# Where the slots of two weight rings begin in the on-chip memory

## The chip, the cores and the metric

The kernel runs on one core of one Trainium2 chip. The metric is the device time of one execution in microseconds (us), from the first to the last instruction and what lies around them. Engines: PE is TensorE, which multiplies (PEld is its loading of the stationary operand), DVE is VectorE, ACT is ScalarE, POOL is GpSimd, SP is SyncE, which here only issues transfers.

## The reference, cut to what matters

The kernel computes four transformer layers in a row on one sequence of 256 rows and width 2048, all in float32: two layers of a first kind (modulated norm, a wide projection, sliding-window attention, spatial gating and gated linear attention side by side, an output projection), then two of a second kind (a wide projection, two attentions, two up projections, an output projection, a layer norm). By far the most arithmetic lies in the projections:

```python
proj = h @ w_in                                   # first kind, twice
out = y @ w_out
h = jnp.einsum('bsd,dc->bsc', x, w_in)            # second kind, twice
up_a = jnp.einsum('bsw,wd->bsd', out_a * jax.nn.silu(za), w_up_a)
up_b = jnp.einsum('bsw,wd->bsd', out_b * jax.nn.silu(zb), w_up_b)
y = jnp.einsum('bsd,de->bse', g_a * up_a + g_b * up_b, w_out)
```

## The kernel before, in words

**The stream of weights.** All projection weights are cut into granules of 128 partitions x 1024 float32 (`GK` = 2 blocks of `CW` = 512 columns; 512 KB each). There are 912 granules: 240 in the first block (`first_block`, from line 1100 on), 672 in the second (`second_block`). Granule n goes through slot n % 4 (`SLOTS`) of three rings in the on-chip memory: SP's queue brings it into `raw` (or, in part of the first block, into `mraw`), ACT rounds it into `whi` (`hi`, L318 and L1414), DVE subtracts to get the rest into `wlo` (`lo`, L435 and L1639), both of type float32r. The activations are split into a high and a low part in the same way (`xhi`, `xlo`, `ahi`, `alo`, `hhi`, `hlo`).

**The products.** For each granule PE runs 12 matmuls (L781 and L2173): high activation by `whi`, low activation by `whi`, high activation by `wlo`, each for two blocks of 128 weight rows and two halves of the 256 sequence rows. In each of them the 128x128 piece of the activation is stationary, and 512 columns of the slot, 2048 bytes on every partition, are the moving operand; the output goes to PSUM and is summed there. So of every 12 matmuls 8 read `whi` and 4 read `wlo`, and 912 x 12 = 10944 matmuls read the two rings.

**What sets the order.** Each engine has its own list of instructions in a fixed order, joined by semaphores: ACT waits for the transfer and for PE's last reading of the slot (`s_used`), DVE waits for ACT (`s_hi`), PE waits for both (`s_hi`, `s_lo`), SP's queue waits for DVE before it refills `raw`. Small attention products and transposes are put between granules by hand (`fills2`, `units2`). Chunk by chunk, PSUM is emptied by ACT and DVE.

**Where things lie.** Tensors are laid out one behind the other in the order of their declarations in `program` (L2274 to L2278). `border` (384 bytes for each partition) brings `x` to a multiple of 512 bytes, and since `x`, `ident`, `raw`, `whi` and `wlo` are multiples of 512 bytes long, all slots begin at multiples of 512. Of the tensors behind the rings, the big ones begin at multiples of 512 too; `sgl` begins 32 bytes behind a multiple of 64.

Of the kernel before, what the change touches and what calls it, by code (L numbers as in the profile page):

```python
# [16 lines left out]
F32 = mybir.dt.float32  # L17
F32R = mybir.dt.float32r
U32 = mybir.dt.uint32
I32 = mybir.dt.int32  # L20
ACT = mybir.ActivationFunctionType
# [3 lines left out]
P = 128  # L25
# [4 lines left out]
CW = 512  # L30
NCW = D // CW
GK = 2
SLOTS = 4
LINE = 128
NEG = -1.0e30
DEPTH = 2

# [12 lines left out]
def at(layer, per_layer, count):  # L50

    return layer * per_layer + count
# [83 lines left out]
def second_block(nc, ctx, x, rings, ps, dram, s_w, ident):  # L136


    raw, whi, wlo = rings
# [7 lines left out]
    def sem(name):  # L147
        return ctx.enter_context(nc.semaphore(name))
# [38 lines left out]
    s_hi = sem("c_hi")  # L187
# [122 lines left out]
    def _(act):  # L310
        act.wait_ge(s_mem, 2)

        for l in range(DEPTH):

            def hi(n, l=l):
                act.wait_ge(s_w[n % SLOTS], at(l, 16 * GRAN2 // SLOTS, 16 * (n // SLOTS + 1)))
                act.wait_ge(s_used, at(l, GRAN2, n + 1))
                act.activation(whi[:, n % SLOTS, :], raw[:, n % SLOTS, :], ACT.Copy).then_inc(s_hi, 1)  # L318

            def fill_hi(name, l=l):  # L320
                h, _, bank = split_views(name)
# [54 lines left out]
            for c in range(nch):  # L376
                prev, j = CHUNKS2[c - 1] if c else (None, None)
                for g in range(granules2(c)):
                    if c == 0 and (l == 0 or g >= LEAD):
                        fill_hi(("x", g))  # L380
                    if c or l == 0 or g > LEAD:
                        hi(FIRST2[c] + g)
                    if (c, g) == (F_CHUNK - 1, 0):

                        act.wait_ge(s_fw, at(l, 32, 32))
                        act.activation(wfhi[:], wf[:], ACT.Copy).then_inc(s_fwh, 1)
                    for grp, r in group_step(c, g):
                        attention(grp, r)
                    if prev == "g" and g == 4:

                        act.wait_ge(*acc_read(l, c - 1))
                        t = (y if j < NCW else gb)[:, :, (j % NCW) * CW:(j % NCW + 1) * CW]
                        act.activation(t, t, ACT.Sigmoid).then_inc(s_gate, 1)
                    if prev == "u" and j >= NCW and g == 5:
                        fill_hi(("y", 2 * (j - NCW)))
                        fill_hi(("y", 2 * (j - NCW) + 1))
                    if (c, g) == (F_CHUNK, 7):

                        act.wait_ge(s_f, l + 1)
                        act.activation(fe[:], fe[:], ACT.Exp).then_inc(s_fln, 1)  # L400
                        act.wait_ge(s_fln, at(l, 2, 1))
                        act.activation(fe[:], fe[:], ACT.Ln, bias=1.0).then_inc(s_fln, 1)
            if l < DEPTH - 1:
                for g in range(LEAD):
                    hi(g, l + 1)
# [5 lines left out]
            if l < DEPTH - 1:  # L411
                hi(LEAD, l + 1)

    @block.vector
    def _(dve):
# [9 lines left out]
        for l in range(DEPTH):  # L425
# [6 lines left out]

            def lo(n, l=l):
                dve.wait_ge(s_hi, at(l, GRAN2, n + 1))
                dve.tensor_tensor(wlo[:, n % SLOTS, :], raw[:, n % SLOTS, :], whi[:, n % SLOTS, :].bitcast(F32),  # L435
                                  ALU.subtract).then_inc(s_lo, 1)

            def fill_lo(name, l=l):
# [51 lines left out]
            def turn():  # L490

                for g in range(LEAD):
                    lo(g, l + 1)
                last_residual(0)
                variance(0)
                inverse_deviation(0)
                normalised(0, 0, CW).then_inc(s_xn, 1)
                last_residual(1)
                fill_lo(("x", 0), l + 1)
                variance(1)  # L500
                inverse_deviation(1)
                normalised(1, 0, CW).then_inc(s_xn, 1)
                link(normalised(0, CW, CW))
                fill_lo(("x", 1), l + 1)
                normalised(1, CW, CW).then_inc(s_xn, 2)
                lo(LEAD, l + 1)
# [123 lines left out]
            for c in range(nch):  # L630
                prev, j = CHUNKS2[c - 1] if c else (None, None)
                for g in range(granules2(c)):
                    if c == 0 and (l == 0 or g >= LEAD):
                        fill_lo(("x", g))
                    if c or l == 0 or g > LEAD:
                        lo(FIRST2[c] + g)
# [218 lines left out]
def rope_tables():  # L855

    half = HD // 2
    inv = (np.float32(10000.0) ** (-np.arange(half, dtype=np.float32) / half)).astype(np.float32)
    ang = (np.arange(SEQ, dtype=np.float32)[:, None] * inv[None, :]).astype(np.float32).astype(np.float64)
    t = np.stack([np.cos(ang), np.sin(ang), -np.sin(ang)])  # L860
    t = np.stack([t * SCALE2, t]).reshape(2, 3, TB, P, half).transpose(3, 0, 1, 2, 4)
    return np.ascontiguousarray(t.astype(np.float32))


def band(weight):

    t, s = np.arange(P)[:, None], np.arange(SEQ)[None, :]
    return np.concatenate([weight(t - s[:, :P]), weight(t + P - s)], axis=1).astype(np.float32)


def constants():
# [5 lines left out]

        "mask_a": band(lambda d: np.where(count(d) > 0, np.log(np.maximum(count(d), 1)), NEG)),
        "mask_b": band(lambda d: np.where(d >= 0, 0.0, NEG)),
        "tables": rope_tables(),  # L880
# [124 lines left out]
def ring_slot(item):  # L1005

    if item in ITEM:
        return ITEM[item] % RING
    return item[1] % SLOTS
# [78 lines left out]
def first_block(nc, ctx, x, rings, ps, dram, ident, s_next=None):  # L1088

    raw, whi, wlo = rings  # L1090
# [7 lines left out]
    def sem(name):  # L1098
        return ctx.enter_context(nc.semaphore(name))
# [59 lines left out]
    s_hi = sem("b_hi")  # L1159
# [142 lines left out]
    def slot(item):  # L1302

        i = ring_slot(item)
        return raw[:, i, :] if i < SLOTS else mraw[:, i - SLOTS, :]

    def landed(item):

        return s_w[ring_slot(item)], 16 * ring_uses(item)
# [99 lines left out]
    def _(act):  # L1409
        def hi(n):  # L1410
            act.wait_ge(*landed(("w", n)))
            if n >= SLOTS:
                act.wait_ge(s_used, n - SLOTS + 1)
            act.activation(whi[:, n % SLOTS, :], slot(("w", n)), ACT.Copy).then_inc(s_hi, 1)  # L1414

        def fill_copy(name, dst, rows=P, n=CW):
            act.wait_ge(*filled(name))
# [68 lines left out]
        for l in range(DEPTH):  # L1486
# [3 lines left out]
            for r in range(GRAN1):  # L1490
                if l and h_fill(l, r) is not None:
                    fill_hi(("h", l, h_fill(l, r)))
                if l == 0 or r >= AHEAD:
                    hi(GRAN1 * l + r)
# [74 lines left out]
                for grp, b in enumerate(R_SWA):  # L1569
                    if 5 <= r - b <= 7:  # L1570
# [3 lines left out]
                        w = P if u == 0 else SEQ  # L1574
                        h0, n = max(0, 2 * (u - 1)), CW // w
# [44 lines left out]
            for r in range(AHEAD if l + 1 < DEPTH else 0):  # L1620
                hi(GRAN1 * (l + 1) + r)
# [6 lines left out]
    def _(dve):  # L1628
# [7 lines left out]

        def lo(n):
            dve.wait_ge(s_hi, n + 1)
            dve.tensor_tensor(wlo[:, n % SLOTS, :], slot(("w", n)), whi[:, n % SLOTS, :].bitcast(F32),  # L1639
                              ALU.subtract).then_inc(s_lo, 1)  # L1640

        def fill_lo(name):
# [170 lines left out]
        for l in range(DEPTH):  # L1813
# [5 lines left out]
            for r in range(GRAN1):  # L1819
# [9 lines left out]
                if l == 0 or r >= AHEAD:  # L1829
                    lo(GRAN1 * l + r)  # L1830
# [135 lines left out]
            for r in range(AHEAD if l + 1 < DEPTH else 0):  # L1966
                lo(GRAN1 * (l + 1) + r)
# [218 lines left out]
def first_constants():  # L2186
# [7 lines left out]
    for m in LEVELS[1:]:  # L2194
# [8 lines left out]
        "lmask": np.stack(masks, axis=1).astype(np.uint8),  # L2203
        "mask_w": band(lambda d: np.where((d >= 0) & (d < WINDOW), 0.0, NEG)),
    }
# [63 lines left out]
def program(nc, dram):  # L2269
    with ExitStack() as ctx:  # L2270
        def sb(name, shape, dt=F32):
            return ctx.enter_context(nc.sbuf_tensor(name, shape, dt))

        sb("border", [P, LINE // 4 * 3])  # L2274
        x = sb("x", [P, TB, D])
        ident = sb("ident", [P, P])
        rings = (sb("raw", [P, SLOTS, GK * CW]), sb("whi", [P, SLOTS, GK * CW], F32R),
                 sb("wlo", [P, SLOTS, GK * CW], F32R))  # L2278
        acc = [ctx.enter_context(nc.psum_tensor(f"acc{i}", [P, TB, CW], F32)) for i in range(2)]
        psT = ctx.enter_context(nc.psum_tensor("psT", [P, TB, CW], F32))  # L2280
        psS = ctx.enter_context(nc.psum_tensor("psS", [P, TB, CW], F32))
        s_w = [ctx.enter_context(nc.semaphore(f"c_w{i}")) for i in range(SLOTS)]
        with ExitStack() as first:
            first_block(nc, first, x, rings, (acc, psT, psS), dram, ident, s_w)
        with ExitStack() as second:
            second_block(nc, second, x, rings, (acc, psT, psS), dram, s_w, ident)
# [22 lines left out]
```

## Time and profile before

| | |
|---|---|
| time of the kernel before, median of 2 runs | 2888.41 us (2887.61 to 2889.22) |
| span of the profiled execution, first to last instruction | 2885.3 us |
| PE busy with matmuls | 2799.2 us, 97% |
| DVE busy | 1792.4 us, 62% |
| ACT busy | 1375.3 us, 48% |
| mean granted TensorE clock | 0.986 |
| read from HBM | 599.41 MB, 208 GB/s over the span |

For the profiled execution the span is known and not a time of its own; the span is 3.1 us shorter than the median of the runs, which is what lies around the instructions. Matmuls overlap in the pipeline of PE: the duration of one is longer than the distance from its start to the next one's start, and it is the distance that counts for the time. The granted clock is 1.00 at 2.4 GHz and 0.50 at 1.2 GHz.

### The profile page before, as it was taken

How to read it: one execution, taken by the hardware profiler on the slowest of the kernel's cores; microseconds unless marked ns; L12 is line 12 of the kernel's file. 1: busy time of each engine (PE TensorE's matmuls, PEld its weight loads, DVE VectorE, ACT ScalarE, POOL GpSimd, SP SyncE). 2: the span in 40 equal slices, each digit the busy share in tenths (PEclk: the TensorE clock that was granted, in tenths of full speed). 3: DMA queues.
4: the chain of work that ended last, by engine and by line, in shares of the span. 5: the costliest groups of instructions: out<-in, count | busy, mean ns of one | idle time of the engine just before them, and what ended most of it. 6: DMA issues, size and time to landing. Idle time of an engine off the chain costs nothing.

```text
span 2885.3 us, 35735 instructions
## 1 busy us (share of the span) xinstructions
PE 2799.2 (97%) x13346; PEld 2318.4 (80%) x13346; DVE 1792.4 (62%) x2195; ACT 1375.3 (48%) x1785; POOL 36.0 (1%) x69
## 2 busy tenths in 40 slices
PE   6799998999998999999999999999999999999998
PEld 5678786888887888888888888878888888888886
DVE  6979898768755555555445556575565545445565
ACT  4355545555544444443545544345445445545443
POOL 0000000000000000000000000000000000000000
PEclk8999999999999999999999999999999999999999
DMA  9987697865554555465554455644555655555564
GB/s 382 354 286 254 208 357 299 314 230 183 201 200 154 173 177 178 160 224 195 177 181 169 173 198 192 222 164 169 176 173 171 224 192 172 179 176 174 197 215 146
DMA packets 159991, 603.73 MB, mean 209 GB/s; under 512 B 18376, under 2 KB 18576, under 8 KB 154464
## 3 DMA queue, kind: packets, MB, share of 16 engines
q1 hardware_dynamic: 155376, 583.08, 57.7%
q0 software_dynamic: 4464, 18.55, 2.1%
q8 instruction: 106, 1.74, 0.2%
q14 instruction: 45, 0.37, 0.0%
HBM read 599.41 MB, written 2.14 MB: 208 GB/s over the span
## 4 chain that ended last, share of the span: by engine, by line
PE 68%; DVE 1%; DMA 0%; ACT 0%; issue 0%; SPq 0%; ACTq 0%; DVEq 0%
PE acc L781 63%; PE psT L729 2%; PE psS L762 1%; PE psS L752 1%; PE psT L735 1%; PE psS L769 0%; DMA raw<-in_w 0%; DVE wlo L435 0%; ACT whi L318 0%; DVE x L488 0%; PE psT L725 0%; DVE x L487 0%; DVE x L469 0%; DVE x L471 0%; DVE stats L454 0%
## 5 line engine op out<-in xcount | busy, mean ns | idle before, releaser
L435 DVE TENSOR_TENSOR wlo<-raw,whi 128x1024 fp32r<-128x1024 f32 x672 | 822.6, 1225 | 866.1 <-ACT whi L318 863.9
L318 ACT ACTIVATE whi<-raw 128x1024 fp32r<-128x1024 f32 x672 | 711.2, 1059 | 995.8 <-PE acc L781 981.7
L781 PE MATMUL acc<-whi,xhi 128*128 128x512 f32 x2304 | 637.8, 398 | 2.5 <-DVE xlo L441 1.5
L781 PE MATMUL acc<-whi,xlo 128*128 128x512 f32 x2304 | 619.4, 390 | 0.0
L781 PE MATMUL acc<-wlo,xhi 128*128 128x512 f32 x2304 | 619.3, 390 | 0.0
L781 PEld LDWEIGHTS acc<-whi,xlo 128*128 128x128 f32 x2304 | 433.1, 188 | 92.4
L781 PEld LDWEIGHTS acc<-wlo,xhi 128*128 128x128 f32 x2304 | 433.1, 188 | 91.5
L781 PEld LDWEIGHTS acc<-whi,xhi 128*128 128x128 f32 x2304 | 422.9, 188 | 83.5 <-DVE xlo L441 3.5
L1414 ACT ACTIVATE whi<-raw 128x1024 fp32r<-128x1024 f32 x177 | 186.9, 1058 | 269.0 <-PE acc L2173 177.7
L2173 PE MATMUL acc<-whi,hhi 128*128 128x512 f32 x864 | 249.5, 411 | 31.3 <-DVE hlo L1650 31.3
L1639 DVE TENSOR_TENSOR wlo<-raw,whi 128x1024 fp32r<-128x1024 f32 x177 | 215.2, 1223 | 90.0 <-ACT whi L1414 89.3
L2173 PE MATMUL acc<-whi,hlo 128*128 128x512 f32 x864 | 238.0, 398 | 0.0
L2173 PE MATMUL acc<-wlo,hhi 128*128 128x512 f32 x864 | 236.5, 396 | 0.0
L2173 PEld LDWEIGHTS acc<-whi,hhi 128*128 128x128 f32 x864 | 159.2, 194 | 69.8 <-DVE hlo L1650 34.8
L2173 PEld LDWEIGHTS acc<-whi,hlo 128*128 128x128 f32 x864 | 166.4, 193 | 36.9
L2173 PEld LDWEIGHTS acc<-wlo,hhi 128*128 128x128 f32 x864 | 165.8, 192 | 35.9
L1414 ACT ACTIVATE whi<-mraw 128x1024 fp32r<-128x1024 f32 x63 | 66.6, 1058 | 81.7 <-PE acc L2173 61.8
L781 PE MATMUL acc<-whi,ahi 128*128 128x512 f32 x384 | 103.2, 391 | 0.0
L781 PE MATMUL acc<-wlo,ahi 128*128 128x512 f32 x384 | 102.7, 389 | 0.0
L781 PE MATMUL acc<-whi,alo 128*128 128x512 f32 x384 | 102.7, 389 | 0.0
L1639 DVE TENSOR_TENSOR wlo<-mraw,whi 128x1024 fp32r<-128x1024 f32 x63 | 77.1, 1223 | 37.7 <-ACT whi L1414 37.5
L1664 DVE SCALAR_TENSOR_TENSOR raw<-raw,crow 128x1024 f32<-128x1024 f32 x79 | 97.1, 1229 | 0.9 <-DMA raw<-in_w_late 0.2
(321 smaller groups left out, 2136.0 us busy)
## 6 DMA issues: line engine op xcount, KB each, us to landing
raw<-in_w SPq DMA_DIRECT2D x849, 512.0 KB, 3.4
raw<-in_w_late SPq DMA_DIRECT2D x79, 512.0 KB, 5.1
mraw<-in_w SPq DMA_DIRECT2D x63, 512.0 KB, 4.8
mraw<-in_w_late SPq DMA_DIRECT2D x49, 512.0 KB, 4.6
b_y<-in_w_early SPq DMA_DIRECT2D x12, 1024.0 KB, 8.4
mraw<-in_w_early SPq DMA_DIRECT2D x7, 1024.0 KB, 8.8
scr<-in_w_early SPq DMA_DIRECT2D x7, 1024.0 KB, 8.8
sgl<-in_w_early SPq DMA_DIRECT2D x6, 1024.0 KB, 9.2
```

Source lines behind the costliest of these rows:

```text
L318: act.activation(whi[:, n % SLOTS, :], raw[:, n % SLOTS, :], ACT.Copy).then_inc(s_hi, 1)
L435: dve.tensor_tensor(wlo[:, n % SLOTS, :], raw[:, n % SLOTS, :], whi[:, n % SLOTS, :].bitcast(F32), ALU.subtract).then_inc(s_lo, 1)
L729: t = pe.transpose(bank[:, k * SEQ + tb * P:k * SEQ + (tb + 1) * P], src[:, tb, col + k * P:col + (k + 1) * P], ident[:])
L735: t = pe.transpose(bank[:, k * P:(k + 1) * P], prob[:, name[2], k * P:(k + 1) * P], ident[:])
L752: m = pe.matmul(out, qT[:, h, tb * P:(tb + 1) * P], kT[:, h, 0:w], start=True, stop=True)
L762: m = pe.matmul(bank[:, h * HD:(h + 1) * HD], probT[:, u, col * P:(col + 1) * P], v[:, s, h * HD:(h + 1) * HD], start=(s == 0), stop=(s == ...
L781: m = pe.matmul(acc[c % 2][:, tb, :], a[:, kk, tb * P:(tb + 1) * P], b[:, n % SLOTS, k * CW:(k + 1) * CW], start=(kk == 0 and q == 0), sto ...
L1414: act.activation(whi[:, n % SLOTS, :], slot(("w", n)), ACT.Copy).then_inc(s_hi, 1)
L1639: dve.tensor_tensor(wlo[:, n % SLOTS, :], slot(("w", n)), whi[:, n % SLOTS, :].bitcast(F32), ALU.subtract).then_inc(s_lo, 1)
L1664: dve.scalar_tensor_tensor(out=slot(("m", i)), in0=slot(("m", i)), scalar=1.0, in1=crow[:, part * MOD_W:(part + 1) * MOD_W], op0=ALU.mult, ...
L2173: m = pe.matmul(bank_a(gc)[:, tb, :], a[:, kt, tile], b[:, n % SLOTS, k * CW:(k + 1) * CW], start=(g == 0 and k == 0 and q == 0), stop=(g ...
```

## The change

Each slot of `whi` and `wlo` becomes 8 bytes longer on every partition (`SHIFT` = 2 float32). Nothing is read or written in these 8 bytes: the two instructions that fill a slot name its first 1024 elements, and the matmuls did so before. So the four slots of `whi` begin 0, 8, 16 and 24 bytes behind a multiple of 512. `whi` as a whole is 32 bytes longer, and the slots of `wlo` begin 32, 40, 48 and 56 bytes behind a multiple of 64. The second half of a slot begins 2048 bytes behind the first, so it has the same place within 64 bytes. A new filler `border_w` of 448 bytes rounds the 64 added bytes up to 512: all that lies behind the rings moves by exactly 512 bytes, and `raw` and what lies ahead of it doesn't move. The instructions of every engine, their order and their waits are the same as before.

```diff
+SHIFT = 2
...
-                act.activation(whi[:, n % SLOTS, :], raw[:, n % SLOTS, :], ACT.Copy).then_inc(s_hi, 1)
+                act.activation(whi[:, n % SLOTS, 0:GK * CW], raw[:, n % SLOTS, :], ACT.Copy).then_inc(s_hi, 1)
...
-                dve.tensor_tensor(wlo[:, n % SLOTS, :], raw[:, n % SLOTS, :], whi[:, n % SLOTS, :].bitcast(F32),
+                dve.tensor_tensor(wlo[:, n % SLOTS, 0:GK * CW], raw[:, n % SLOTS, :], whi[:, n % SLOTS, 0:GK * CW].bitcast(F32),
                                   ALU.subtract).then_inc(s_lo, 1)
...
-            act.activation(whi[:, n % SLOTS, :], slot(("w", n)), ACT.Copy).then_inc(s_hi, 1)
+            act.activation(whi[:, n % SLOTS, 0:GK * CW], slot(("w", n)), ACT.Copy).then_inc(s_hi, 1)
...
-            dve.tensor_tensor(wlo[:, n % SLOTS, :], slot(("w", n)), whi[:, n % SLOTS, :].bitcast(F32),
+            dve.tensor_tensor(wlo[:, n % SLOTS, 0:GK * CW], slot(("w", n)), whi[:, n % SLOTS, 0:GK * CW].bitcast(F32),
                               ALU.subtract).then_inc(s_lo, 1)
...
-        rings = (sb("raw", [P, SLOTS, GK * CW]), sb("whi", [P, SLOTS, GK * CW], F32R),
-                 sb("wlo", [P, SLOTS, GK * CW], F32R))
+        rings = (sb("raw", [P, SLOTS, GK * CW]), sb("whi", [P, SLOTS, GK * CW + SHIFT], F32R),
+                 sb("wlo", [P, SLOTS, GK * CW + SHIFT], F32R))
+        sb("border_w", [P, 112])
```

## Rows read from the trace of the kernel before

**Rows 1.** The page: busy time of the engines, and the granted clock by slices

```profile
PE 2799.2 (97%) x13346; PEld 2318.4 (80%) x13346; DVE 1792.4 (62%) x2195; ACT 1375.3 (48%) x1785; POOL 36.0 (1%) x69
...
PEclk8999999999999999999999999999999999999999
```

**Rows 2.** The page: the chain that ended last, by engine

```profile
PE 68%; DVE 1%; DMA 0%; ACT 0%; issue 0%; SPq 0%; ACTq 0%; DVEq 0%
```

**Rows 3.** Groups by line: PE matmuls on the rings (count; busy us, mean ns)

```profile
L781 PE MATMUL acc<-whi,xhi 128*128 128x512 f32 x2304 | 637.8, 398 | 2.5 <-DVE xlo L441 1.5 <-ACT whi L318 0.9
...
L2173 PE MATMUL acc<-whi,hhi 128*128 128x512 f32 x864 | 249.5, 411 | 31.3 <-DVE hlo L1650 31.3
...
L781 PE MATMUL acc<-whi,ahi 128*128 128x512 f32 x384 | 103.2, 391 | 0.0
...
L2173 PE MATMUL psS<-whi,hhi 128*128 128x512 f32 x64 | 17.1, 389 | 0.0
...
L2173 PE MATMUL psT<-whi,hhi 128*128 128x512 f32 x32 | 8.6, 389 | 0.0
```

**Rows 4.** Chain in order of time, 2200 to 2400 us: start, length, what

```profile
2209.01 163.23 PE acc L781 x720
```

**Rows 5.** Windows: length, busy us (instructions) of each engine, clock, DMA share, GB/s

```profile
0.00:165.00 165.00, 122.50 (x466) 95.49 (x467) 128.11 (x157) 67.72 (x86) 11.49 (x24) 0.89 0.92 359
165.00:500.00 335.00, 316.96 (x1682) 262.14 (x1681) 295.40 (x493) 177.20 (x287) 6.91 (x12) 0.97 0.78 279
...
2211.00:2371.00 160.00, 160.00 (x708) 132.53 (x707) 83.50 (x74) 73.10 (x70) 2.70 (x5) 1.00 0.61 203
...
67.90:71.80 3.90, 3.90 (x10) 2.97 (x9) 3.52 (x15) 0.00 (x0) 0.00 (x0) 0.50 0.88 346
```

**Rows 6.** Timeline of PE at granted clock 0.50: start us, us, what

```profile
69.24 1.91 PE L2173 MATMUL acc<-whi,hlo 128*128 128x512 f32 x4
70.95 1.87 PE L2173 MATMUL acc<-wlo,hhi 128*128 128x512 f32 x4
72.65 1.09 PE L2173 MATMUL acc<-whi,hhi 128*128 128x512 f32 x4
```

**Rows 7.** Timeline of PE: matmuls of 256 moving float32r columns

```profile
2205.56 0.28 PE L769 MATMUL psS<-xhi,wflo 128*12 128x256 f32 x1
...
2208.73 0.28 PE L769 MATMUL psS<-xlo,wfhi 128*12 128x256 f32 x1
```

**Rows 8.** Timeline, 2300 to 2306 us: one granule in its turn

```profile
2301.35 1.07 PE L781 MATMUL acc<-whi,ahi 128*128 128x512 f32 x4
...
2301.61 1.06 ACT L318 ACTIVATE whi<-raw 128x1024 fp32r<-128x1024 f32 x1 [1.66 <-PE acc L781]
...
2302.70 1.23 DVE L435 TENSOR_TENSOR wlo<-raw,whi 128x1024 fp32r<-128x1024 f32 x1 [1.49 <-ACT whi L318]
...
2304.07 1.07 PE L781 MATMUL acc<-whi,ahi 128*128 128x512 f32 x4
```

**Rows 9.** Groups by line: DVE and ACT on slots, and DVE on sgl

```profile
L435 DVE TENSOR_TENSOR wlo<-raw,whi 128x1024 fp32r<-128x1024 f32 x672 | 822.6, 1225 | 866.1 <-ACT whi L318 863.9
L1639 DVE TENSOR_TENSOR wlo<-raw,whi 128x1024 fp32r<-128x1024 f32 x177 | 215.2, 1223 | 90.0 <-ACT whi L1414 89.3
...
L1919 DVE TENSOR_TENSOR b_stage<-b_stage,sgl 128x1024 f32<-128x1024 f32 x2 | 2.5, 1226 | 0.1
...
L1657 DVE SCALAR_TENSOR_TENSOR mraw<-mraw,crow 128x2048 f32<-128x2048 f32 x7 | 16.0, 2288 | 0.0
L1657 DVE SCALAR_TENSOR_TENSOR sgl<-sgl,crow 128x2048 f32<-128x2048 f32 x6 | 13.7, 2288 | 0.0
```

**Rows 10.** Groups by line: ACT on the slots

```profile
L318 ACT ACTIVATE whi<-raw 128x1024 fp32r<-128x1024 f32 x672 | 711.2, 1059 | 995.8 <-PE acc L781 981.7 <-DMA raw<-in_w 14.0
```

## The prediction

> **What bounds the kernel now.** I read the page first: PE is busy for 2799.2 us of a span of 2885.3 us, 97%, and the granted clock is nearly full throughout [rows 1]. The chain that ended last is PE's wherever it can be put down to an engine [rows 2]. No other engine comes near: DVE is at 62%, ACT at 48%. Then I asked what PE spends its time on. The groups by line give the counts: 2304, 864, 384, 64 and 32 matmuls of the kind high activation by `whi`, 3648 together [rows 3], and as many of each of the two other kinds, so 10944. Each streams 512 columns out of a slot of `whi` or `wlo`. All that the change can do to the bound lies in how long one of these streams takes.
>
> The duration in the group rows, 390 to 411 ns, is a latency and not the price. The price is the distance between starts. The chain in order of time has a piece of 720 such matmuls with nothing between them in 163.23 us, 226.7 ns each, or 2.72 us for a granule of 12 [rows 4, 8]. 10944 x 226.7 ns is 2481 us, 86% of the span.
>
> Is 226.7 ns the array's pace or that of the operand? 512 columns at 2.4 GHz are 213.3 ns, so there are 13.3 ns (32 cycles) too many. At half the granted clock [rows 5] the starts of fours stand 1.71 and 1.70 us apart [rows 6], 426 ns for one, which is 512 columns at 1.2 GHz and nothing on top. And with 256 moving columns and only 12 stationary ones, 28 starts take 3.17 us [rows 7], 113.2 ns each, where 256 columns at 2.4 GHz are 106.7. The excess is a sixteenth in both, it grows with the columns streamed, it doesn't come from loading the stationary operand, and it is gone when the array asks at half the pace. So I read it as the supply of the moving operand: at full clock PE gets 2048 bytes in 226.7 ns, that is 64 bytes (16 elements) in 7.08 ns where the array would take them in 6.67. The supply binds, with no slack to hide a dearer read. This is why a matter of 8 bytes has to be priced at all.
>
> **The change part by part.** The added bytes are not touched, no instruction is added or moved, the waits and the transfers into `raw` are the same, and everything behind the rings moves by a whole 512 bytes: all of that costs 0.
>
> *ACT and DVE on shifted slots.* ACT writes `whi`, DVE reads it and writes `wlo`, now at odd places in a line. The trace has one tensor off a multiple of 64, `sgl`, 32 bytes behind one. DVE with `sgl` as an operand takes 1226 ns for 1024 elements, and 1223 to 1225 with slots; over 2048 elements, where it also writes `sgl`, 2288 ns against 2288 on `mraw` [rows 9]. I take 0. There is no such row for ACT, nor for 8 bytes; the cover that would hide a cost is that in the steady stretch DVE works 83.5 us and ACT 73.1 us of 160 [rows 5, 8]. The subtraction would have to cost 1.3 us more (76.5 us of idle over 59 granules), over double of today's 1.23, before PE waited. Only between 165 and 500 us is DVE at 88% (295.4 of 335): 5% on each subtraction there, 0.06 us on some 123 granules, would be 7 us at most. The 1.06 us of ACT [rows 10] ahead of DVE have the same cover.
>
> *PE's streams.* Slots are used in turn, 228 granules each. `whi` is read 8 times a granule: 1824 matmuls for each slot, at 0, 8, 16 and 24 bytes. `wlo` is read 4 times: 912 for each, at 32, 40, 48 and 56. Off a multiple of 64 are 3 x 1824 + 4 x 912 = 9120 matmuls, five in six. Of these, 5472 begin 8 behind a multiple of 16 (two slots of each ring), and 8208 are off a multiple of 32. No row of the trace has a moving operand off 64 bytes, so the cost of one is bounded from the rows nearest. Below: 0, the supply counts elements or 8-byte words and doesn't know lines. Above, without a new kind of stall: a stream that begins inside a 64-byte line touches 33 lines and not 32, and if the part-used line costs as much as a whole one, that is 226.7 / 32 = 7.08 ns. In between lies the reading that I find nearest to the row of 16 + 1 cycles: the extra cycle is a turn at each line's end, and what is read of a line costs by its elements. Then 33 turns take the place of 32: one cycle, 0.42 ns; if the line is 128 bytes and the turn two cycles of 2.4 GHz, 0.83 ns. 9120 x 0.42 = 3.8 us, 9120 x 0.83 = 7.6 us.
>
> **The sum.** 2885.3 + 3.8 = 2889 us of span; with the 3.1 us by which the median of the runs stands above the profiled span, 2892 us.
>
> One rule speaks against the change. The Trainium skill, page "SBUF — State Buffer", section "Door 1: The DMA port swizzle", says that the memory has lines of 16 bytes, that two accesses to a line are needed to hide its latency, and that each access which crosses to a new line pays a penalty. It gives no price; its measurements of operands at odd starts (section "Operand start alignment") are by its own words about legality and not speed. No run here shows the size of a line.
>
> **The rivals.**
>
> *Whole small lines.* If the supply fetches lines of 16 bytes and always pays for a whole one, a stream that begins 8 behind a multiple of 16 needs 129 for 128: 226.7 / 128 = 1.77 ns on 5472 matmuls, 9.7 us, 2898 us. With lines of 32 bytes it is 3.54 ns on 8208, 29.1 us, 2917 us. For it: the supply binds, so whatever it fetches more must show. Against it: a line fetched whole should let the next one's first elements wait in a buffer, and a fetch that is part idle needn't cost the same. Chance 0.12. The 16-byte form is how that rule of the Trainium skill would act here.
>
> *Whole lines of 64 bytes* (the other side). Place: the start of each of the 9120 streams; price 7.08 ns each, 64.6 us. Some of it falls where PE isn't the bound: PE is idle 60.5 us in the first 500 us, the home of about a seventh of the matmuls [rows 5]. With up to a tenth absorbed it is 58 to 65 us: 2947 to 2953 us, slower by 2.0 to 2.2%. It decides from 6.4 ns for each shifted stream on (58 us), so at about one whole 64-byte fetch. For it: sixteen elements and one lost cycle is a 64-byte rhythm, and there is no slack. Against it: nothing in the rows says that a part costs as much as the whole. Chance 0.14.
>
> *Every fetch straddles.* If PE asks for 16 elements at a time counted from the operand's start, each request touches two lines and pays the turn twice: 13.3 ns more for a stream, 121 us, 3010 us (if 128-byte lines are meant and one is lost whole, 14.2 ns and 129 us). For: the same excess of 13.3 ns is there today, and there would be one more of it. Against: a prefetcher of a sequential stream has no need to ask twice for a line. Chance 0.08.
>
> *The excess goes away.* If the sixteenth comes from aligned reads of two operands meeting, shifted slots would avoid it: at most 13.3 ns x 9120 = 121 us faster, 2767 us. Against it, the row with 12 stationary columns has the same sixteenth [rows 7], and so few stationary reads can hardly meet so many moving ones. Chance 0.03.
>
> *ACT or DVE dearer*, up to the 7 us worked out above: 2896 us. Chance 0.03.
>
> **How the numbers follow.** The forecast has 0.60: 2892 us, its own range 2886 to 2897. About 2%, 58 us, is what is counted here as different from no change. Within it lie the forecast, the whole small lines and the dearer ACT or DVE: 0.60 + 0.12 + 0.03 = 0.75. Slower by over 2% are the 64-byte lines and the straddling: 0.14 + 0.08 = 0.22. Faster: 0.03. Forecast and small lines alone would leave out a quarter, so the range reaches up to the end of the 64-byte case: 2884 to 2954 us. It leaves out 0.08 above and 0.03 below, and some of each case's own spread.
>
> **What would show it.** The steady stretch near 2210 us: 720 matmuls take 163.2 us in every case that costs nothing, 163.5 us with one cycle on five in six, 167.5 with 7.08 ns, 171.2 with 13.3. Slots differ: with turns alone slot 0's `whi` streams keep 226.7 ns and all others stand at 227.1; with 16-byte lines only slots 1 and 3 are slower; with 64-byte lines all but slot 0 of `whi`. At half clock 426 ns should stay whatever happens, if the supply is the cause. The subtractions should stay at 1223 to 1226 ns and ACT at 1059. I am wrong if the steady distance differs from 226.7 by over a nanosecond, or if the time moves while it doesn't.

## The result and the profile after

The changed kernel takes 2935.99 us (median of 2 runs, 2935.18 to 2936.80), 47.6 us more than before: ratio 1.0166, 95% interval 1.0149 to 1.0182. That is inside the range and on the slower side of the forecast of 2892 us, 44 us above it.

The page of the changed kernel, with span, busy times and chain, to be held against [rows 1] and [rows 2]:

```profile
span 2935.1 us, 35735 instructions
...
PE 2849.2 (97%) x13346; PEld 2327.1 (79%) x13346; DVE 1792.2 (61%) x2195; ACT 1376.3 (47%) x1785; POOL 36.7 (1%) x69
...
PE 68%; DVE 1%; DMA 0%; ACT 0%; issue 0%; SPq 0%; ACTq 0%; DVEq 0%
```

The span grew by 49.8 us and PE's busy time by 50.0; DVE and ACT work as long as before. All of it is PE. (The span grew by more than the median time because the profiled executions aren't the median ones. In every run that has both numbers, the time is only 1.7 to 1.8 us above the span: of the 3.1 us between the median before and the profiled span, about half is the spread of the runs and doesn't lie around the instructions. The forecast of 2892 us doesn't change by that.) The groups by line of DVE and ACT on the slots (one line later now) answer to [rows 9, 10]: 1225, 1222 and 1061 ns where 1225, 1223 and 1059 stood.

```profile
L436 DVE TENSOR_TENSOR wlo<-raw,whi 128x1024 fp32r<-128x1024 f32 x672 | 822.5, 1225 | 902.9 <-ACT whi L319 900.9
L319 ACT ACTIVATE whi<-raw 128x1024 fp32r<-128x1024 f32 x672 | 712.2, 1061 | 1032.7 <-PE acc L782 1017.7 <-DMA raw<-in_w 14.8
...
L1640 DVE TENSOR_TENSOR wlo<-raw,whi 128x1024 fp32r<-128x1024 f32 x177 | 215.1, 1222 | 95.1 <-ACT whi L1415 94.3
```

The chain in order of time has the same piece of 720 streams as [rows 4]:

```profile
2245.24 167.02 PE acc L782 x720
```

167.02 us for 163.23: 232.0 ns a stream for 226.7. The timeline of PE in this piece (start, length, what; the distance is the difference of two starts, over 4) shows which slots pay:

```profile
2287.76 1.10 PE L782 MATMUL acc<-whi,xlo 128*128 128x512 f32 x4
2288.70 1.10 PE L782 MATMUL acc<-wlo,xhi 128*128 128x512 f32 x4
2289.64 1.07 PE L782 MATMUL acc<-whi,xhi 128*128 128x512 f32 x4
2290.55 1.07 PE L782 MATMUL acc<-whi,xlo 128*128 128x512 f32 x4
2291.45 1.10 PE L782 MATMUL acc<-wlo,xhi 128*128 128x512 f32 x4
2292.39 1.09 PE L782 MATMUL acc<-whi,xhi 128*128 128x512 f32 x4
2293.32 1.09 PE L782 MATMUL acc<-whi,xlo 128*128 128x512 f32 x4
2294.25 1.10 PE L782 MATMUL acc<-wlo,xhi 128*128 128x512 f32 x4
```

The third and fourth row are slot 0 of `whi`, at a multiple of 512: 0.91 and 0.90 us for four, 227 ns. The first two `wlo` rows (56 bytes in slot 3, 32 in slot 0) take 0.94 us, 235 ns; the two rows before the last are slot 1 of `whi`, at 8 bytes, 0.93 us, 233 ns.

From the starts of all matmuls in the trace: where two streams of the rings follow one another within 260 ns (10,300 places in both kernels), the distances exceed 226.67 ns by 7.8 us in all before and by 57.2 us after. The difference, 49.4 us, is the whole growth of the span. The 7.8 us that stood there before all lie in the first nine streams behind a pause or a product of another kind. At its longest the series of distances is 235, 233, 236, 224, 231, 236, 228, 233, 231, then 226.7 until the next such place; in other places it begins further on in the same series.

### The profile page after: what moved, and what is told of

Read it like the earlier page. It is cut to its first block, busy times and chain, and to the rows that moved or that the text cites. A ratio compares the mean times of both kernels' runs of the same rounds, so it can differ in the third digit from the quotient of the medians.

```text
span 2935.1 us, 35735 instructions
## 1 busy us (share of the span) xinstructions
PE 2849.2 (97%) x13346; PEld 2327.1 (79%) x13346; DVE 1792.2 (61%) x2195; ACT 1376.3 (47%) x1785; POOL 36.7 (1%) x69
## 4 chain that ended last, share of the span: by engine, by line
PE 68%; DVE 1%; DMA 0%; ACT 0%; issue 0%; SPq 0%; ACTq 0%; DVEq 0%
PE acc L782 63%; PE psT L730 1%; PE psS L763 1%; PE psS L753 1%; PE psT L736 1%; PE psS L770 0%; DMA raw<-in_w 0%; DVE wlo L436 0%; DVE x L472 0%; DVE x L470 0%; ACT whi L319 0%; DVE x L489 0%; DVE x L488 0%; PE psT L726 0%; DVE stats L455 0%
## 5 line engine op out<-in xcount | busy, mean ns | idle before, releaser
L436 DVE TENSOR_TENSOR wlo<-raw,whi 128x1024 fp32r<-128x1024 f32 x672 | 822.5, 1225 | 902.9 <-ACT whi L319 900.9
L319 ACT ACTIVATE whi<-raw 128x1024 fp32r<-128x1024 f32 x672 | 712.2, 1061 | 1032.7 <-PE acc L782 1017.7
L782 PE MATMUL acc<-whi,xhi 128*128 128x512 f32 x2304 | 645.0, 401 | 2.5 <-DVE xlo L442 1.5
L782 PE MATMUL acc<-wlo,xhi 128*128 128x512 f32 x2304 | 633.7, 396 | 0.0
L782 PE MATMUL acc<-whi,xlo 128*128 128x512 f32 x2304 | 629.1, 394 | 0.0
L1640 DVE TENSOR_TENSOR wlo<-raw,whi 128x1024 fp32r<-128x1024 f32 x177 | 215.1, 1222 | 95.1 <-ACT whi L1415 94.3
```

The lines of the kernel that those rows point to most:

```text
L319: act.activation(whi[:, n % SLOTS, 0:GK * CW], raw[:, n % SLOTS, :], ACT.Copy).then_inc(s_hi, 1)
L436: dve.tensor_tensor(wlo[:, n % SLOTS, 0:GK * CW], raw[:, n % SLOTS, :], whi[:, n % SLOTS, 0:GK * CW].bitcast(F32), ALU.subtract).then_inc( ...
L782: m = pe.matmul(acc[c % 2][:, tb, :], a[:, kk, tb * P:(tb + 1) * P], b[:, n % SLOTS, k * CW:(k + 1) * CW], start=(kk == 0 and q == 0), sto ...
L1640: dve.tensor_tensor(wlo[:, n % SLOTS, 0:GK * CW], slot(("w", n)), whi[:, n % SLOTS, 0:GK * CW].bitcast(F32), ALU.subtract).then_inc(s_lo, 1)
```

## The experiments

Theories: **A**, a stream that begins inside a 64-byte line pays for an extra line, by itself. **B**, it is the place of the stream to that of the stationary operand being loaded that counts. **C**, it is the change from one place to another between streams. In all kernels a small class hands out the slots by a table of starts, which moves the lines of the code by 11 (the class and the line that names `raw` are left out below); the table is the edit. Each timed kernel was compared with the kernel before on the same chip.

### All slots at one odd place

```diff
-        rings = (sb("raw", ...), sb("whi", [P, SLOTS, GK * CW], F32R), sb("wlo", [P, SLOTS, GK * CW], F32R))
+        rings = (raw, Ring(sb("whi", [P, 4128], F32R), [8, 1032, 2056, 3080]),   # second kernel: [2, 1026, 2050, 3074]
+                 Ring(sb("wlo", [P, 4128], F32R), [8, 1032, 2056, 3080]))
+        sb("border_w", [P, 64])
```

> All slots of both rings begin 32 bytes behind a multiple of 128 (instead of 0 before, and of eight different places after). In the changed kernel the steady stretch of 720 matmuls took 167.02 us for 163.23, and the slots off a multiple of 64 stood at 229 to 238 ns for 226.7. Theory A (a stream that begins inside a 64-byte line costs a nearly whole line more, wherever it begins and whatever the stationary operand does): one constant distance of about 233 ns for all 12 matmuls of a granule, 720 in 168 us, time 2888 + 10944 x 6 to 7 ns, about 2955 us. Theory B (the cost comes from streams and stationary loads, or successive streams, standing at different places in a line; a lock is lost): distances vary from matmul to matmul as in the changed kernel, mean depends on the offset. Theory C (the changing from one offset to another is what costs): 226.7 ns, 2888 us.

> All slots begin 8 bytes behind a multiple of 128. Theory A: the same as with 32 bytes, about 233 ns and 2955 us. If the cost goes by lines of 32 bytes as well, or grows with the offset (in the changed kernel whi at 8 to 24 bytes stood at 231.2 to 232.6 ns on average, wlo at 32 to 56 bytes at 233.5 to 235.2), it is about 232 ns and 2940 us, less than with 32. Theory C: 2888 us.

`whi` of 4128 elements is 128 bytes longer than a multiple of 512, so `wlo`'s slots stand 128 bytes further: the slots are at 32 (`whi`) and 160 (`wlo`) behind a multiple of 512, in the second kernel at 8 and 136. Below they are called by 32 and 8.

Measured: 2951.72 us at 32 bytes (ratio 1.0222, 1.0205 to 1.0239) and 2954.19 us at 8 (1.0231, 1.0213 to 1.0248). The piece of 720 streams, at 32 bytes and then at 8:

```profile
2255.47 168.37 PE acc L792 x720
```

```profile
2257.77 168.40 PE acc L792 x720
```

233.8 and 233.9 ns. C falls in the form that a changing place within a line of 64 or 128 bytes is what costs: none changes here, and the price is the full one. (Between `whi` and `wlo` the place still changes by 128 bytes; the kernel below with only the stationary operands moved has no change of any kind among the streams and loses 57 us.) A's sizes are met, but not its constant: in the kernel at 32 bytes single distances run from 230 to 238 ns. At half clock (granted 0.50) the shifted streams cost nothing; timeline of PE at 32 bytes:

```profile
85.83 1.91 PE L2184 MATMUL acc<-whi,hlo 128*128 128x512 f32 x4
87.54 1.35 PE L2184 MATMUL acc<-wlo,hhi 128*128 128x512 f32 x4
```

1.71 us for four, as in [rows 6]. In the changed kernel a four of `wlo` at half clock takes 1.71 us too (starts at 70.21 and 71.92 us).

### Slots at multiples of 64

```diff
+        rings = (raw, Ring(sb("whi", [P, 4160], F32R), [0, 1040, 2080, 3120]),
+                 Ring(sb("wlo", [P, 4160], F32R), [0, 1040, 2080, 3120]))
```

> Slots are spaced like in the changed kernel, but by 64 bytes instead of 8: whi at 0, 64, 128, 192, wlo at 256, 320, 384, 448 bytes behind a multiple of 512. Theory A with a line of 64 bytes: 226.7 ns everywhere, 2888 us. If the line is 128 bytes long, slots 1 and 3 of both rings (half of the matmuls) pay some 6 to 14 ns: 2920 to 2965 us, and slots 0 and 2 nothing. Theory C (different offsets of successive streams): some cost in each granule's first matmuls of a kind.

Measured: 2927.49 us, ratio 1.0138 (1.0121 to 1.0155). No stream begins inside a 64-byte line, and yet 40 us are lost. By slot, in steady granules: slot 0 (`whi` at 0, `wlo` at 256) is at 226.7 ns but for its first five streams, `wlo` included; slot 1 (64, 320) is at 226 to 232 from its fifth stream on; slots 2 (128, 384) and 3 (192, 448) stand at 232.9 on average. So not slots 1 and 3, as a 128-byte line would have it. That `wlo` at 256 bytes is free points to a period of 256 bytes, which the kernel "256 bytes apart" tests.

### Only the stationary operands moved

```diff
+        rings = (raw, Ring(sb("whi", [P, 4096], F32R), [0, 1024, 2048, 3072]),
+                 Ring(sb("wlo", [P, 4096], F32R), [0, 1024, 2048, 3072]))
+        sb("border_w", [P, 8])
```

> The slots stay at multiples of 512, and all that lies behind the rings begins 32 bytes behind a multiple of 64: the stationary operands of all big matmuls (hhi, hlo, xhi, xlo, ahi, alo), and the 256 moving columns of L769 and L2084. Theory A: 226.7 ns for the big matmuls, time 2888 us; the 256-column matmuls with only 12 or 16 stationary columns, whose moving operand is now off a line, go from 113.3 to about 120 ns (192 of them, 1 us in all). Theory B (it is the places of the two operands to one another that count): the big matmuls stand at 229 to 238 ns, time 2930 to 2960 us.

Measured: 2944.04 us, ratio 1.0194 (1.0177 to 1.0211). Chain of this kernel in order of time:

```profile
2245.10 5.47 PE psS L780 x48
2250.57 168.00 PE acc L792 x720
```

Every stream of the rings is at a multiple of 512 bytes here, as before, and takes 233.3 ns. The 48 matmuls with 256 moving columns, whose moving operand is now 32 bytes off and whose stationary one has 12 columns, take 5.47 us, 114.0 ns each. Chain of the kernel before, the same 48:

```profile
2203.54 5.46 PE psS L769 x48
```

In that shape a stream off a line pays nothing, and in the big matmuls a stream on a line pays 6.6 ns because the other operand was moved: A is dead, and my reading of the price as one of the moving operand's supply with it. By the profile it is the stream that gets longer here, not the load: from 2300 to 2380 us a load of the stationary operand takes 188 ns as in the kernel before, a matmul 396 ns for 389.

### Both moved together

```diff
+        rings = (raw, Ring(sb("whi", [P, 4104], F32R), [8, 1032, 2056, 3080]),
+                 Ring(sb("wlo", [P, 4096], F32R), [0, 1024, 2048, 3072]))
```

`wlo` and all behind it then begin 32 bytes behind a multiple of 512 because `whi` is 32 bytes longer.

> Both kinds of operand begin 32 bytes behind a multiple of 512: all slots of whi and wlo, and all that lies behind the rings (the stationary operands), so that moving and stationary operand stand as in the kernel before to one another. Slots alone at 32 and 160 bytes cost 65 us, stationary operands alone at 32 bytes 57 us. Theory B (it is the place of the stream to that of the stationary operand that counts, as if the two reads met in the same part of the memory): 226.7 ns again, 720 matmuls in 163.2 us, 2888 us. Theory A (each read off a line pays by itself): both costs, 2888 + 65 + 57, at least 2950 us.

Measured: 2886.43 us, ratio 0.9997 (0.9988 to 1.0007). A shift of the slots by 32 bytes (65 us, there with `wlo` at 160) and one of the stationary operands by 32 (57 us) cost nothing together. At 32 bytes a stream off a 64-byte line is free if its partner stands there too:

```profile
2211.69 163.23 PE acc L792 x720
```

### 256 bytes apart

```diff
+        rings = (raw, Ring(sb("whi", [P, 4160], F32R), [64, 1088, 2112, 3136]),
+                 Ring(sb("wlo", [P, 4096], F32R), [0, 1024, 2048, 3072]))
+        sb("border_w", [P, 64])
```

> All slots of both rings begin 256 bytes behind a multiple of 512; the stationary operands stay at multiples of 512. With slots at multiples of 64 bytes the wlo streams at 256 behind whi streams at 0 stood at 226.7 ns, those at 64 and 320 bytes at 226 to 232, those at 128, 192, 384 and 448 at 228 to 241. Theory B with a period of 256 bytes: 226.7 ns, 2888 us. If the period is 512 bytes, or if the free place was only carried over from the streams ahead, 230 to 235 ns and 2930 to 2960 us.

Measured: 2888.32 us, ratio 0.9997 (0.9988 to 1.0007), and the 720 streams as in the kernel before:

```profile
2211.07 163.23 PE acc L792 x720
```

### A ladder of lone matmuls

Behind the last output, after `pe.wait_ge(s_fin, len(PIECES))`, one line for each group (o, t in float32, w stationary columns, n moving ones):

```diff
+            for i in range(32): pe.matmul(ps_s[0:w, 0, 0:n], still(t, i, w), flow(o, n), start=True, stop=True)
```

`flow` reads `whi` from element o on, `still` reads `xhi` from t + 128 (i % 4) on.

> The kernel before, and behind its last output 32 groups of 32 matmuls each, alone on the chip with no ACT, DVE or transfer beside them, each group with the moving operand (512 columns, in two groups 256) at one place behind a multiple of 512 bytes and the stationary one (128 columns, in five groups 12) at another; their results are read by nobody. About 230 us longer than before. Theory B: at equal places, at 256 apart and with 12 stationary columns 226.7 ns for each (7.25 us for a group); at other distances between the two operands 228 to 238 ns, the same for the same distance whichever of the two is moved. Theory A: all groups off a multiple of 64 at about 233 ns, with 12 stationary columns as well. If ACT's and DVE's accesses to the rings are the cause: 226.7 ns in all groups, since neither works here.

One run, 3118.72 us. The chain in order of time gives a group's length; divided by 32 it is the price, with the first streams of the group in it. Here L867 to L874 are streams at 8, 16, 24, 32, 48, 64, 96 and 128 bytes with the stationary operand at 0, L866 one at 4; L878 and L879 are 256 and 320; L884 is both at 32, L886 the stationary operand at 8 and the stream at 0, L887 both at 8, L889 both at 128; L890 and L892 have 12 stationary columns and streams at 0 and 32; L895 and L896 have 256 moving columns at 0 and 32.

```profile
2894.37 7.57 PE psS L866 x32
2901.94 7.46 PE psS L867 x32
2909.40 7.41 PE psS L868 x32
...
2924.28 7.46 PE psS L870 x32
...
2939.20 7.32 PE psS L872 x32
...
2953.99 7.44 PE psS L874 x32
...
2983.83 7.26 PE psS L878 x32
...
3028.06 7.26 PE psS L884 x32
...
3042.58 7.39 PE psS L886 x32
3049.97 7.40 PE psS L887 x32
...
3064.80 7.25 PE psS L889 x32
3072.05 7.41 PE psS L890 x32
...
3086.90 7.42 PE psS L892 x32
...
3109.13 3.83 PE psS L895 x32
3112.96 3.77 PE psS L896 x32
```

From the starts of the matmuls, without the first ones of a group, the mean distances are, by how far the stream's start lies behind the stationary operand's, which is at a multiple of 512:

| bytes | 0 | 4 | 8 | 16 | 24 | 32 | 48 | 64 | 96 | 128 | 160 | 192 | 224 | 256 | 320 | 384 | 448 | 512 |
|---|---|---|---|---|---|---|---|---|---|---|---|---|---|---|---|---|---|---|
| ns | 226.7 | 236.7 | 233.5 | 231.6 | 233.3 | 233.3 | 233.4 | 229.0 | 233.2 | 232.3 | 234.3 | 233.4 | 233.4 | 226.7 | 229.0 | 232.4 | 233.4 | 226.7 |

The row from 256 on repeats the one from 0 on. With the stationary operand at 32 or 128 bytes and the stream at 0 it is 233.4 and 232.0 to 232.4, as at 224 and 128: for multiples of 32 bytes the distance decides, whichever of the two is moved. ACT, DVE and transfers are at rest here, so they have no part in it. Two expectations of B missed: both at 8 bytes costs 231.1, not 226.7, and with 12 stationary columns it is 231 to 232 wherever the stream begins, 0 included. And with 256 moving columns (128 stationary) the order is turned round: 120.0 ns at distance 0, 117.8 at 32.

### A second ladder

> A second ladder of 32 groups of 32 matmuls behind the last output, results read by nobody. In the first, the same distance between the operands gave the same price (226.7 ns at 0 and 256 bytes), but both at 8 bytes gave 231.1 and 12 stationary columns 231 to 232 ns wherever the stream began. If only the distance counted, both at 4, 16, 24, 48, 64, 96 bytes would give 226.7 ns; if the distance counts and lines of 32 bytes have to be kept as well, 4, 8, 16, 24 and 48 are dear and 64 and 96 free. With 1 to 96 stationary columns at distance 0: if loads that are shorter meet fewer reads, the price falls to 226.7 ns or to 213.3 plus little at 1 column; if a short load loses the step in which the two reads go beside each other, it stands at 229 to 233 ns for all but 128 columns, and at 32 bytes of distance likewise. With one stationary piece for all 32 matmuls (step 0) in place of four in turn: the same as with four.

One run, 3108.02 us; the same edit with other places. L867 is both at 4 bytes, L872 both at 64, L873 both at 96; L878 and L884 have 1 and 96 stationary columns at distance 0; L887 has 96 at distance 32; L890 and L891 have one stationary piece throughout, at distance 0 and 32; L894 and L895 have 384 moving columns, at 0 and 32.

```profile
2895.74 7.60 PE psS L867 x32
...
2933.02 7.28 PE psS L872 x32
2940.30 7.29 PE psS L873 x32
...
2977.25 7.33 PE psS L878 x32
...
3021.41 7.37 PE psS L884 x32
...
3043.61 7.25 PE psS L887 x32
...
3065.66 7.29 PE psS L890 x32
3072.94 7.47 PE psS L891 x32
...
3087.69 5.55 PE psS L894 x32
3093.24 5.55 PE psS L895 x32
```

Equal places off a multiple of 32 bytes cost too: both at 4 bytes 238.0 ns when settled, at 8, 16 and 48 bytes 231.1, at 24 bytes 233.4; at 64 and 96 bytes 226.7. That is the second reading named ahead: the distance counts, and multiples of 32 bytes have to be kept as well. Whether a place off 32 bytes costs through one operand alone isn't told apart by these groups. Which distance is free depends on the stationary length as well: with 96 columns distance 0 costs 230.0 and distance 32 is free. With 384 moving columns the two distances cost the same, 173.3 ns. That the stationary piece is another each time doesn't matter. So it isn't a plain count of meeting reads, which shorter loads would lower. It looks like a rhythm into which the two reads of successive matmuls fall or fail to fall; that isn't shown, and what sets it stays open. Nor is it shown that the load of the next stationary piece is what meets the stream: every matmul has a load beside it.

The ladders also answer a premise of the prediction. With 128 stationary columns at distance 0, matmuls of 256, 384 and 512 moving columns cost 120.0, 173.3 and 226.7 ns, and these columns at 2.4 GHz are 106.7, 160.0 and 213.3 ns. The excess is 13.3 ns in all three: a fixed amount for a matmul, not a sixteenth of its columns.

### One part of the change: only wlo shifted

```diff
+        rings = (raw, Ring(sb("whi", [P, 4096], F32R), [0, 1024, 2048, 3072]),
+                 Ring(sb("wlo", [P, 4112], F32R), [8, 1034, 2060, 3086]))
+        sb("border_w", [P, 112])
```

> One part of the change alone: whi's slots stay at multiples of 512, wlo's begin 32, 40, 48 and 56 bytes behind one, as in the changed kernel. Theory B now: each stream whose distance to the stationary operand isn't a multiple of 256 bytes pays 4.5 to 8.5 ns, the others nothing. Then the 3648 wlo streams pay about 7 ns, 26 us, and the whi streams stand at 226.7 ns but for the first ones behind a wlo stream: 2912 to 2920 us. If a shifted stream also disturbs those behind it for long, all 12 matmuls of a granule are dearer and the time is near that of the changed kernel, 2936 us.

Measured: 2928.20 us, ratio 1.0144 (1.0127 to 1.0161). Between the two answers, and above the 2912 to 2920 us of prices added up one by one. A third of the streams is shifted, and 39.6 us of excess are there where the whole change has 49.4. In the steady granules of slots 0 to 2 the eight `whi` streams, all at multiples of 512, stand at 224 to 236 ns, in an order that was there behind other products before (236, 224, 231, 236, 228); only in slot 3 are they back at 226.7 after two. Timeline of PE:

```profile
2308.26 1.09 PE L792 MATMUL acc<-whi,alo 128*128 128x512 f32 x4
2309.19 1.09 PE L792 MATMUL acc<-wlo,ahi 128*128 128x512 f32 x4
2310.11 1.10 PE L792 MATMUL acc<-whi,ahi 128*128 128x512 f32 x4
2311.05 1.08 PE L792 MATMUL acc<-whi,alo 128*128 128x512 f32 x4
2311.97 0.40 PE L792 MATMUL acc<-wlo,ahi 128*128 128x512 f32 x1
```

`whi` takes 0.93, 0.94 and 0.92 us for four here. A dear stream can make those behind it dear, here for all eight. In the ladders streams at free places behind a dear group were back at 226.7 after one to seven.

### Do the ladder's prices hold in the kernel?

```diff
+        rings = (raw, Ring(sb("whi", [P, 4160], F32R), [1, 1025, 2049, 3073]),   # second kernel: [16, 1040, 2064, 3088]
+                 Ring(sb("wlo", [P, 4160], F32R), [1, 1025, 2049, 3073]))
```

> All slots of both rings begin 4 bytes behind a multiple of 256, stationary operands at multiples of 512. The ladder of lone matmuls gave 236.65 ns for this distance, the dearest of its row. If its prices hold in the kernel (theory B, by distance to the stationary operand), the steady stretch of 720 takes 170.4 us and the kernel 2888 + 10944 x 10.0 ns = 2997 us, at most some us less where PE isn't the bound or runs at half clock. If instead all places off 32 bytes cost about the same in the kernel (as 8 and 32 bytes did: 2954 and 2952 us), 2950 to 2960 us.

> All slots begin 64 bytes behind a multiple of 256. The ladder gave 229.0 ns for this distance: 720 matmuls in 164.9 us, 2888 + 10944 x 2.35 ns = 2914 us. If the prices of the ladder don't carry over (other blocks, ACT and DVE at work beside it): 226.7 ns and 2888 us, or about 233 ns and 2955 us.

Measured: 2984.23 us (ratio 1.0338, 1.0320 to 1.0355) at 4 bytes and 2906.39 us (1.0061, 1.0045 to 1.0078) at 64. The 720 streams at 4 bytes, then at 64:

```profile
2279.13 170.38 PE acc L792 x720
```

```profile
2222.97 164.80 PE acc L792 x720
```

The ladder had said 170.4 and 164.9 us. The whole times are 13 and 8 us below the expectation. Of the 10944 streams some 630 aren't followed by another within 260 ns (another product, a pause or half clock lies between), and 7.8 us of excess were already there before. Taken off, that leaves 95 and 16 us by the ladder's prices; the excess grew by 97.3 and 17.4 us, the medians by 95.9 and 18.0.

The ladder's table can now be laid against the change itself. An estimate for the 720 streams, each at the price of its place, two thirds `whi` and one third `wlo` (for 40 and 56 bytes, which the ladder doesn't have, the 233.4 ns of 48): 231.98 ns on average, 167.0 us, and 167.02 were measured. For the slots at 32 and 160 bytes it gives 168.2 us (measured 168.37), for those at multiples of 64 165.9 (166.41), and with only `wlo` shifted 164.8, where the chain in order of time has more:

```profile
2238.09 166.59 PE acc L792 x720
```

The more free streams stand behind dear ones, the more the sum of single prices falls short.

## Why the prediction was right or wrong

**The bound** was right: PE, through the distance between streams, and nothing else moved.

**ACT and DVE at 0** was right: 1225, 1222 and 1061 ns, for 8 bytes and for ACT too, which no row had shown. **The transfers, the waits and the move by 512 bytes at 0** was right as well.

**PE's streams** is the step that failed. Put at 0.42 ns on each of 9120 shifted streams (3.8 us), it was 49.4 us, 5.4 ns for each. The choice of the streams as the place of the cost was right, the kind of cost wasn't. I had priced a longer fetch of the moving operand alone. The runs with only the stationary operands moved (+57 us) and with both moved together (0) show that the pair counts. I had bounded the cost "without a new kind of stall", and the pair of reads was just such a kind. Both runs moved by 32 bytes, the place of slot 0 of `wlo` in the change. Six of the eight slots are off a multiple of 32 bytes besides, and at such places even equal starts cost 4.4 ns or more in the ladders; how much of the price of these six comes from the distance and how much from that isn't separated.

**The argument that led me off** was the one on the 256-column matmuls. They showed an excess of a sixteenth with 12 stationary columns, from which I took it that the excess grows with the columns streamed and that the stationary operand has no part. I had compared two shapes that differ in both operands. In the ladders, 12 columns with 512 moving ones cost 231 to 232 ns, 256 moving columns cost 113.3 ns with 64 stationary columns and 120.0 with 128, and with 128 stationary columns the excess is 13.3 ns at 256, 384 and 512 moving ones. So the rate of 64 bytes in 7.08 ns, on which the forecast and the rivals with lines were built, doesn't describe the floor.

**The rivals.** That the time lies within the range is luck. The range reached so far up only for the rival of whole 64-byte lines (chance 0.14), 2947 to 2953 us, 11 to 17 us too high and for a reason that was refuted: slots at multiples of 64 lost 40 us, both operands at 32 bytes nothing, and single slots weren't at a constant price. Its 167.5 us for the steady stretch came close to the 167.02 measured, by chance too. The rule on 16-byte lines of the Trainium skill (page "SBUF — State Buffer", section "Door 1: The DMA port swizzle") doesn't decide it either: 64 and 128 bytes are whole lines and cost 2.3 and 5.6 ns. Nor did only slots 1 and 3 get slower, as the rival with 16-byte lines had it: slot 2 of `whi`, at 16 bytes, stands at 231.3 ns on average in the changed kernel. The rival in which the two operands' reads meet was there, but with the opposite sign: I let alignment be the meeting and the shift the cure. That shifted could be the worse place of the two should have had a chance of its own, with a price from the streams behind other products, which stood at 224 to 236 ns in the trace before. I had read only the steady stretch; up to nine such streams in a row with aligned operands were the one sight in the trace before of dearer distances at full clock.

Against the finding stands another statement of the Trainium skill (page "TensorE: Matmul & The Clock Gate", section "Step-by-step: what each phase is for"): that PE reads its moving and its stationary operand through two independent ports, so that loading the next weights takes nothing from the running matmul. For float32r streams of 512 columns with 128 stationary ones at full clock the runs disagree in so far as the two reads aren't without effect on one another: leaving the slots and moving what is loaded made the streams dearer by 6.6 ns each, and the worst pair of places in the ladders is 11 ns above 226.7.

**The signs named ahead.** Half clock stayed at 427 ns and slot 0 of `whi` at 226.7 but for its first stream, as said; neither sign told the supply from the pair of places. The distance in the steady stretch rose by 5.3 ns, over the one nanosecond from which I had called myself wrong.

## What to carry to other kernels

In a kernel bound by a dense stream of float32r matmuls with 128 stationary and 512 moving columns, keep the start of the moving and of the stationary operand a multiple of 256 bytes apart and each at a multiple of 32: here that is 0 against 18 to 96 us of 2888. It is no rule for other shapes: with 96 stationary columns a distance of 32 bytes was the cheaper one, with 256 moving columns also (117.8 ns against 120.0), and with 384 it made no difference. A pad of some bytes between slots, or a small tensor declared ahead of a big one, is enough to lose it, and moving both by the same multiple of 32 bytes is enough to get it back. And don't take an excess for a rate from two shapes that differ in both operands: change one at a time. To find out who pays, read the distance between starts of a long even stretch, and price places with a ladder of lone matmuls behind the kernel: where all streams stand at like places it foretold the steady stretch within 0.1%, and with only `wlo` shifted it fell 1.8 us of 166.6 short.

## What the runs showed of the hardware that was not expected

- Where the stationary operand begins changes the price of the stream: 226.7 ns at distances of 0, 256 and 512 bytes, 229.0 at 64 and 320, 231.6 to 234.3 at most others, 236.7 at 4 bytes (128 stationary, 512 moving float32r columns, clock granted in full).
- Both operands at the same place off 32 bytes cost as well: 231.1 ns at 8, 16 and 48 bytes, 238.0 at 4.
- The dearer distances outlast their cause by up to nine matmuls. Behind a shifted stream, a pause or a product of another kind, aligned streams run at 224 to 236 ns before they are back at 226.7.
- At half clock none of this was seen: 427 ns, at 0 bytes and at 32.
- No group came below 226.7 ns for 512 columns, not with one stationary column either (about 229). With 128 stationary columns the floor is 13.3 ns above the time of the columns at 2.4 GHz at 256, 384 and 512 of them alike. What sets it is open; at half clock it isn't there.
